# Expert weight chunks in two transfers of 1 MB with a semaphore each, and their products in row-first order

## What is computed

```python
def expert_choice_ffn(x, router_w, wg, wu, wd):
    cap = CAPACITY_FACTOR * n // N_EXPERTS                      # 32
    aff = softmax(einsum('bnd,de->bne', x, router_w))
    gate, idx = top_k(aff.transpose(0, 2, 1), cap)
    xg = x[bidx, idx]
    hid = silu(einsum('becd,edf->becf', xg, wg)) * einsum('becd,edf->becf', xg, wu)
    o = einsum('becf,efd->becd', hid, wd) * gate[..., None]
    return zeros_like(x).at[bidx, idx].add(o)
```

## Time and profile before

| | us |
|---|---|
| median of 3 runs | 3087.09 (3083.38 to 3089.05) |
| the profiled execution | 3091.27 |
| its span, first to last instruction | 3089.3 |
| PE busy | 2848.0 (92%) |
| DVE busy | 968.5 (31%) |
| ACT busy | 535.5 (17%) |
| mean granted PE clock | 0.953 |

### The profile page before, as it was taken

How to read it: one execution, slowest core, us unless ns; L and a number is a source line. 1 busy time by engine, 2 the same in 40 slices (tenths; PEclk the granted TensorE clock), 3 DMA queues, 4 the chain that set the end, 5 groups by cost and what they waited for, 6 DMA issues and landing times.

```text
span 3089.3 us, 32473 instructions
## 1 busy us (share of the span) xinstructions
PE 2848.0 (92%) x13332; PEld 1710.2 (55%) x13332; DVE 968.5 (31%) x1944; ACT 535.5 (17%) x1073; POOL 74.8 (2%) x125
## 2 busy tenths in 40 slices
PE   7998889999989998888777999999999999999998
PEld 3455554444335564432323776675874776674883
DVE  2545432222225453111121425342001434343001
ACT  1143211111101331101110222310000213310000
POOL 2100000000001000000000000000000000000000
PEclk9999889999999988888898999999999999999999
DMA  9314259999996348999999432234444332224341
GB/s 286 111 56 152 82 199 382 409 409 409 409 401 210 112 152 329 408 409 409 409 409 355 148 118 89 82 104 144 146 147 157 136 109 102 89 90 156 136 150 68
DMA packets 237442, 670.29 MB, mean 217 GB/s; under 512 B 8112, under 2 KB 18664, under 8 KB 237296
## 3 DMA queue, kind: packets, MB, share of 16 engines
q1 hardware_dynamic: 230480, 653.28, 56.2%
q0 software_dynamic: 6816, 14.94, 2.0%
HBM read 667.09 MB, written 2.90 MB: 217 GB/s over the span
## 4 chain that ended last, share of the span: by engine, by line
PE 69%; DMA 20%; DVE 5%; SPq 3%; ACT 2%; issue 1%; POOL 0%; DVEq 0%; ACTq 0%; POOLq 0%
PE bank L856 32%; DMA ring<-in_exp_w_up_dram 19%; PE bank L1436 8%; PE bank L868 8%; PE bank L1454 5%; PE bank L1077 3%; PE bank L313 3%; SPq L558 2%; PE bank L1129 1%; PE bank L1016 1%; PE bank L1277 1%; PE bank L1038 1%; PE bank L898 1%; PE bank L824 1%; PE bank L1116 1%
## 5 line engine op out<-in xcount | busy, mean ns | idle before, releaser
L868 PE MATMUL bank<-ring,arena 128*64 128x512 f32 (+1 forms) x2992 | 604.6, 645 | 122.8 <-DMA ring<-in_exp_w_up_dram 98.3
L856 PE MATMUL bank<-arena,ring 128*128 128x256 f32 (+1 forms) x2496 | 530.1, 374 | 0.6 <-ACT arena L414 0.6
L856 PEld LDWEIGHTS bank<-arena,ring 128*128 128x128 f32 x2496 | 463.9, 190 | 67.1 <-ACT arena L414 1.1
L856 PE MATMUL bank<-ring,arena 128*128 128x512 f32 (+1 forms) x1116 | 468.5, 580 | 4.3 <-DVE arena L2845 1.7
L868 PEld LDWEIGHTS bank<-ring,arena 128*64 128x64 f32 (+1 forms) x2992 | 174.9, 129 | 531.8 <-issue 427.5
L856 PEld LDWEIGHTS bank<-ring,arena 128*128 128x128 f32 x1116 | 210.8, 190 | 251.8 <-issue 247.4
L1436 PE MATMUL bank<-ring,arena 128*128 128x512 f32 x640 | 295.5, 593 | 0.0
L1454 PEld LDWEIGHTS bank<-ring 128*128 128x128 f32 x1248 | 154.0, 192 | 42.0 <-issue 37.3
L2523 DVE COPY arena<-bank 128x512 f32<-128x512 f32 x64 | 44.3, 692 | 406.1 <-PE bank L868 405.1
L1436 PEld LDWEIGHTS bank<-ring,arena 128*128 128x128 f32 x640 | 112.0, 191 | 92.8 <-issue 92.8
L1454 PE MATMUL bank<-ring 128*128 128x128 f32 x1248 | 155.9, 275 | 2.1 <-DVE ring L2785 2.1
(11 more groups left out here) (293 smaller groups left out, 2312.3 us busy)
## 6 DMA issues: line engine op xcount, KB each, us to landing
ring<-in_exp_w_down_dram SPq DMA_DIRECT2D x64, 2048.0 KB, 20.6
ring<-in_exp_w_up_dram SPq DMA_DIRECT2D x63, 2048.0 KB, 23.8
ring<-in_exp_w_gate_dram SPq DMA_DIRECT2D x60, 2048.0 KB, 23.6
ring<-in_w_in_dram SPq DMA_DIRECT2D x42, 2048.0 KB, 7.8
ring<-in_ada_w_dram SPq DMA_DIRECT2D x24, 2048.0 KB, 10.3
ring<-in_w_ffn_up_dram SPq DMA_DIRECT2D x20, 2048.0 KB, 7.9
ring<-in_w_out_dram SPq DMA_DIRECT2D x8, 2048.0 KB, 9.7
ring<-in_w_ffn_down_dram SPq DMA_DIRECT2D x8, 2048.0 KB, 7.8
```

What stands on the lines that cost most here:

```text
L856: last = mm(o, lhs(k), rhs(k), start=start and k == 0, stop=stop and k == kt - 1)
L868: last = mm(U(us[c])[g * rows:(g + 1) * rows, :], lhs(k), rhs(i, c), start=(k < parts), stop=(k >= KT - parts))
```

## The change

It has three parts. A chunk that goes through `expert_load` is loaded by two transfers of 1 MB, row tiles 0 and 1 on `chunk{s}` and row tiles 2 and 3 on a new semaphore `chunk_rest{s}`. `next_expert` waits for the first as before and notes the second, for which PE waits ahead of row tile 2. In `halved` the loops are swapped: row tiles outside, the two column halves inside, so that the products run (i0,c0), (i0,c1), (i1,c0), (i1,c1) and so on. The banks are counted as full at the last row tile. Chunks in the spare places keep their loads and have no second wait, but their products take the new order too.

```diff
             def expert_load(l, q):
 
                 s = EXPERT_SLOTS[l][ring_turn(l, q) % RING]
-                eng.dma_start(wide[s], expert_rows_of(l, q)).then_inc(sem[f"chunk{s}"], 16)
+                for i, landed in enumerate(("chunk", "chunk_rest")):
+                    rows = slice(2 * i, 2 * i + 2)
+                    eng.dma_start(wide[s][:, rows, :], expert_rows_of(l, q)[:, rows, :]).then_inc(sem[f"{landed}{s}"], 16)
...
         def next_expert(l):
...
+                rest[0] = None
                 return [part[:, i, :] for part in extra_parts(x) for i in range(part.shape[1])]
...
+            rest[0] = f"chunk_rest{s}"
             return [wide[s][:, i, :] for i in range(4)]
...
         def halved(us, rows, lhs, rhs, half, parts):
 
-            for c in range(2):
-                for i in range(KT // 2):
+            for i in range(KT // 2):
+                if i == 2 and rest[0]:
+                    nc.tensor.wait_ge(sem[rest[0]], pe.due(rest[0], 16))
+                for c in range(2):
                     k = half * (KT // 2) + i
                     g = k % parts
                     last = mm(U(us[c])[g * rows:(g + 1) * rows, :], lhs(k), rhs(i, c), start=(k < parts), stop=(k >= KT - parts))
                     if pending[0]:
                         last.then_inc(sem["chunk_used"], 1)
                         pending[0] = 0
-                if half == 1:
-                    last.then_inc(full[us[c] % BANKS], 1)
+                    if half == 1 and i == KT // 2 - 1:
+                        last.then_inc(full[us[c] % BANKS], 1)
```

More of the change, by code:

```diff
@@ L208, in build @@
         names += [f"chunk{s}" for s in range(RING)]
-        names += [f"extra{x}" for x in range(max(EXTRA))]
+        names += [f"extra{x}" for x in range(max(EXTRA))] + [f"chunk_rest{s}" for s in range(RING)]
         names += ["chunk_used", "vector_step", "scalar_step", "rows_in", "tokens_in", "consts", "smalls", "band_out", "bias_in",
@@ L782, in next_chunk @@
             return s
+        rest = [None]
         def next_expert(l):
```

## The result

The changed kernel has a median of 3092.5 us over 12 runs, the kernel before 3085.24 over as many: 7.3 us more, a ratio of 1.0025 with a 95% interval of 1.0014 to 1.0036. I had forecast 1.5 us less. The time lies in the range, but its sign is the other one. One of the twelve runs of each, 4129.58 us before and 3439.70 us after, was in a slow state and stays out of the ratio. The profiled executions are 3097.47 us (span 3095.7, granted clock 0.955) and 3091.27 us (3089.3, 0.953).

What follows compares the result with a forecast made beforehand. The middles of both expert stages were taken as bound by transfer rate, PE bounding the stream's start and the stage ends. Terms +0.3 +0.2 -0.76 +0.5 -1.7 = -1.5 us, from 3087.1 to 3085.6; range 3079 to 3095.

Steps and rivals of the forecast that it cites:

- The transfers: Ring chunk loads: 187 transfers of 2 MB become 374 of 1 MB at no visible cost, +0.3 us, at most 1.9.
- PE's rate in the new order: Expert products: column groups still run abreast, so no change, 3.43 us for a chunk at two groups, 1.72 at four.
- The folds: After the up chunks: first-layer folds start 0.1 us later each, +0.2 at the stream's start; second layer +0.
- The down chunks: Ends of both expert stages: c = 0 done 0.86 us later, costing +0.86 in the first layer, +0.5 in the second.
- The early half: Last up chunk: row tiles 0 and 1 done before the rest lands, -1.72 us in the first layer, 0 in the second.
- The clock: Last up chunk of the first layer: its half-clock loss avoided, -1.7 us; other clock losses left where they are.
- The groups run abreast: Rival denied here: only one record of a group can wait, groups no longer run abreast, 3099.8 us; chance 0.10.
- the clock in the first layer's middle: Rival: two stretches of half clock per expert make PE the bound there, 3095 us; chance 0.06.
- the split costs: Rival: fixed transfer price paid in line, 2.8 us for each of 187, +520 us, or a share; chance 0.03.
- both ends were not freed of low clock: Rival denied here: all low-clock losses at both layers' ends avoided, 3079.3 us; chance 0.10.
- the halves land one after the other: Opposite of a rival: both halves served side by side, first lands no earlier, 3089 us; chance 0.08.

Runs made afterwards that it cites:

- e1: Kernel before with each chunk split into two 1 MB transfers, PE waiting for both, products in the old order: 3085.8 us against 3083.57, ratio 1.0003.
- e9: Kernel before, whole transfers, with product (0, 1) moved ahead of (3, 0) in each matrix's second chunk: 3087.65 us, one run.
- e5: Kernel before with split transfers; gate and up of the first layer fill c = 0 then c = 1 within each landed half, the rest old order: 3083.89 us, 0.9996.
- e3: Changed kernel with column halves outside again within each landed half of a chunk: 3084.73 us, ratio 0.9997 against the kernel before.
- b0: The kernel before, unchanged, run again: 3086.03 us against 3083.57 of the same text, ratio 1.0009.
- c1: The changed kernel, unchanged, run again: 3089.71 us against 3083.57 for the kernel before, ratio 1.0016.
- e2: Changed kernel without the split: whole 2 MB transfers, new product order: 3093.53 us, ratio 1.0027 against the kernel before.
- e6: Kernel before, whole transfers, with the new order in the first layer alone: 3090.19 us, ratio 1.0021.
- e7: Kernel before, whole transfers, with the new order in the second layer alone: 3090.01 us against 3082.97, ratio 1.0017.
- e4: Changed kernel with the new order only in each matrix's first chunk, old order in the second, transfers split: 3082.34 us, 0.9996 against the kernel before.
- e8: Kernel before, whole transfers, row tiles taken 0, 2, 1, 3 with column halves inside, so eight records of a group in a row: 3107.94 us, one run.

## Why the prediction was wrong

**The transfers: right.** The middles run at 409 GB/s, and a chunk's landing follows the last one's by 5.12 us, in the median of the first layer's middle, in the split kernels as before; e1's ratio is 1.0003, with 1.0016 as the upper end. My +0.3 can't be told from 0. The Trainium skill, "DMA: Bandwidth & Descriptors", section "Anatomy of one DMA", gives about 2.0 us fixed for each transfer on the GpSimd path. Paid in line by 187 more transfers, which is my estimate and not the page's, these would be 374 us, and e1 rules that out.

**PE's rate in the new order: right.** x16 takes 3.7 us, and the changed kernel's chain has x96 at 20.80 (20.75 in the earlier trace rows):

```profile
489.34 3.76 PE bank L1285 x32
493.09 3.63 PE bank L1237 x32
496.72 20.80 PE bank L876 x96
517.52 0.86 issue
```

**The folds: this step failed.** The prediction says of the bank of c = 0: "now it is full one product, 0.86 us (two steps), ahead of the end". The products are done then, but the bank is signalled only at the end, for the reason that e9 isolates. My 0.1 us for each fold is 0.9. The rows above show it: from fold to fold it is 517.52 + 0.86 - 489.34 = 29.04 us in the changed kernel and 28.09 in the kernel before, while PE is the chain. I counted two such folds ahead of the point where the queue fills: +1.9 at most instead of +0.2. For the second layer I had written "fold +0", and it is +0.9 too.

The earlier trace rows couldn't have told me: there the copy of c = 0 (907.49) follows the end of its last product in program order at once, which any rule fits, since A and B take turns. But the trace of the kernel before could, 3 us behind the place of the earlier trace rows, where groups C and D run ahead of A and B. The record that fills the gate's bank of c = 0 ends at 1235.55, and the copy starts 0.95 us later:

```profile
1236.50 0.59 ACT L1853 COPY arena<-bank 128x512 f32<-128x512 f32 x1 [2.02 <-PE bank L868]
```

The semaphore's update stands at 1236.42, 0.87 us after that record. So I took from these rows that records may overtake, and did not look at when the overtaking ones signal. The Trainium skill, "TensorE: Matmul & The Clock Gate", section "Part 3: Packing small matmuls", says that "MATMULs are pc-monotone in start AND end". I had weighed the half on starts, which the earlier trace rows contradict, and dropped the half on ends with it; the ends as the records give them contradict it too (908.40 ahead of 909.24), but the signals obey it. By it the folds would have been forecast at +0.9.

**The down chunks: the same step.** I had the column half c = 0 done 0.86 us later than before; its signal is 1.7 us later in the first layer, since it used to be four steps ahead of the end and is now at it. In the second layer the net I gave was +0.5, and PE's wait ahead of L1256 grew by 3.04 - 1.61 = 1.4.

**The early half: right in size for the first layer.** -1.72 was forecast, 1.6 to 1.7 measured in e5 and e3. It is earned once, at the end of the layer. The signals are paid at every fold that PE is the bound for. For the second layer I had written that it saves 0. By steps it does, but the clock was higher there, as told below.

**The clock: right that some comes back, wrong in the place.** I took 1.7 us as gained, since the last up chunk of the first layer ran at 0.50. It ran at full clock in the changed kernel, but also in b0 and e1, where the order is the old one: from landing to fold 5.32 us in the profiled kernel before, 3.63 and 3.72 in these. It was a trait of one execution and not of the order.

The loss that the change does avoid is one that I had left where it was, in the last up chunk of the second layer. PE had idled 3.11 us ahead of it and it took 3.35 us, with a granted clock of 0.55. In the changed kernel PE idles 0.64 us and each portion takes 1.92 at 1.00. The same holds in c1 and e3, the other two kernels in which PE does half of each chunk's work in that layer on the chunk's first half. In all ten other traces that chunk ran mostly at half clock and took 3.2 to 3.6 us. From the landing of the last up chunk to the fold it is 3.3 to 3.6 us in before, b0 and e1, 2.9 in the changed kernel and c1 in spite of the late signal, and 2.0 in e3. So the end of the second layer gained 0.4 to 0.7 us there instead of losing 0.9.

Over all runs the mean granted clock is 0.953 or 0.954 for the kernel before, 0.953 in e1, 0.959 and 0.960 for the changed kernel and c1, 0.967 in e3, and 0.946 to 0.949 in e2, e6 and e7. Most of that is the second layer's middle (0.86 before, 0.93 in the changed kernel, 0.82 in e2, 0.97 in e3, from 1300 to 1600 us), which runs at 409 GB/s either way. So the mean clock doesn't explain the time: the changed kernel has more of it than the kernel before and is slower.

There is low clock elsewhere. In the second layer, at the start of its experts, the changed kernel has:

```profile
1244.19 3.75 PE L1285 MATMUL bank<-arena 128*128 128x32 f32 x32 [0.89 <-issue]
1247.76 3.66 PE L1237 MATMUL bank<-arena 128*128 128x128 f32 x16
```

The gather took 2.03 us before. The window over it shows why, and the window of e1's gather beside it:

```profile
1247.80:1251.30 3.50, 3.50 (x18) 3.42 (x17) 1.67 (x3) 0.28 (x1) 0.56 (x1) 0.52 1.03 411
```

```profile
1239.10:1241.00 1.90, 1.90 (x19) 1.78 (x19) 1.25 (x3) 0.28 (x1) 0.00 (x0) 1.00 1.01 403
```

It took 3.36 to 3.66 us in six traces in which this fold had idled 0.9 us (the changed kernel, c1, e2, e3, e7, e9), 2.03 in before, b0, e1 and e5, where it hadn't, but also 3.15 in e6 and 3.18 in e4, where it hadn't either. The gather behind the next fold was slow (3.60 to 3.76 us) in before, e1, e4, e5 and e6 too, with no idle fold. So the idle time went with the slow gather at this one place; that it causes it is not shown.

**The rivals.** None of the five that I named explains the time. The groups run abreast; the clock in the first layer's middle is 0.99, and 0.95 in c1, where the stage still runs at 409 GB/s; the split costs nothing that shows; both ends were not freed of low clock; and the halves land one after the other, or PE would not have had two portions. The slower case that did come, a signal that is later than the work, wasn't among them. (In the working of my first rival, the column groups, 8 x 1.72 + 2 x 0.86 is 15.5 and not 15.4, which changes nothing.)

**The sum again, with what was measured.** Start of the first layer: +1.0 to +1.9 (one or two folds). Its end: -1.72 + 0.95 + 1.72 = +0.95. Start of the second: from its first expert product to the landing of its last up chunk it is 446.9 us before, 447.7 in the changed kernel and 449.9 in c1, so +0.8 to +2.9. Its end: -0.4 to -0.7 with the clock, and +1.4, so +0.7 to +1.0. After the experts, see below: +0.5 to +2.9. Together that is +4 to +10, against a measured +7.3 between the medians and +6.1 in c1. A sum as wide as this agrees with the loss, but doesn't prove that it is complete. For the single pair of profiles (+6.2 us) it can't be made term by term: 2.4 us of it stood already before the first expert product, where nothing is changed, and the mixes of low clock differ.

**What stays open.** After its last expert product the second layer has 1412.4 to 1412.8 us to go in all six traces with the old order there (before, b0, e1, e5, e6, and e4, whose second chunks have it), and 1414.6 to 1417.2 in the seven with another (the changed kernel, c1, e2, e3, e7, e9, e8). Up to PE's 16th record after it that is 6.3 us against 6.8 to 8.7. The late signal is 1.4 us of this (0.6 in e3, e8 and e9), and the rest is low clock right behind it, which c1 doesn't have. Later, where the instructions are the same, another 0.5 us comes up in c1 and 1.9 to 2.4 in the six others. The low clock takes 20.8 us of this whole stretch in each of the first six traces, 27.5 in c1 and 31 to 35 in the six others. Why a shift at the stage's end moves the low clock so far behind it, no run here tells. e3 has this too, about 3 us in all, and its time is not above that of the kernel before. Nor was a kernel tried that moves the signals alone, with the products where they are. So that the signals are late is shown, and that the order costs the time is shown; that the late signals make up all of that time is not.

Nothing that ran beats the kernel before: e3, e4 and e5 lie 0.03 to 0.04% under it, with intervals of 0.1%.

## What to carry to other kernels

When products of several column groups are interleaved, look at which ones stand ahead of the signalling product in program order, not at when its own group is done: put all that fills a bank ahead of what fills the next, or the signal waits for the others. Where records of one column group overtake those of another, look at when the overtaking ones signal, before you count on it. An early start on half a transfer is worth its wait once, at the end of a stage that is bound by transfers; whatever it costs at each fold is paid wherever PE is the bound. And a stretch of low clock seen in one profile of before belongs in the range and not in the forecast, until a second profile has it at the same place.

## What the runs showed of the hardware

- TensorE's signals come in program order across column groups: 0.92 us from the end of the signalling record to the copy with one product of another group ahead, 0.1 without (e9 and the kernel before). The kernel before shows it too where C and D overtake A and B: 0.95 us (1235.55 to 1236.50).
- A record can start ahead of four records of another group that stand ahead of it in program order, and no more: the fifth is passed only once the first has ended (e8, 20 steps for two chunks that need 16).
- Splitting transfers of 2 MB, with rows of 4 KB, into 1 MB each leaves a full stream at 409 GB/s, 187 times (e1, 1.0003).
- The last up chunk of the second layer ran at a granted clock of 1.00 in the three traces in which PE had idled 0.65 us or less ahead of it and worked in two portions (the changed kernel, c1, e3), and mostly at half clock in the ten others, with idle times of 1.4 to 3.2 us ahead of it.
